# RWKV chunk inversion: odd chunks swap the heads' halves at each product, and the inverse is built from factors of one plus a power

## What is computed

```python
def step(s, inp):
    r_t, w_t, k_t, v_t, a_t, b_t = inp
    sa = jnp.einsum('bhij,bhj->bhi', s, a_t)
    s = s * w_t[:, :, None, :] + sa[..., None] * b_t[:, :, None, :] + v_t[..., None] * k_t[:, :, None, :]
    return s, jnp.einsum('bhij,bhj->bhi', s, r_t)
```

## Time and profile before

| what | value |
|---|---|
| median of 3 runs | 4082.98 us |
| range of the 3 runs | 4081.25 to 4083.41 us |
| profiled execution, own time | 4082.34 us |
| span of the profiled execution | 4080.1 us |
| instructions in the span | 84733 |
| PE busy, share of the span | 94% |
| DVE busy, share of the span | 58% |
| ACT busy, share of the span | 38% |

### The profile page before, as it was taken

The page is one execution under the profiler, slowest core; times in us unless marked ns, Lnnn a source line. Parts: engine busy times, 40 slices in busy tenths (PEclk is TensorE's granted clock), DMA queues, the critical chain, the costliest instruction groups (busy, mean ns, idle before and its releaser), DMA issues. The chain is left out here.

```text
span 4080.1 us, 84733 instructions
## 1 busy us (share of the span) xinstructions
PE 3834.2 (94%) x35926; PEld 3513.7 (86%) x35926; DVE 2363.4 (58%) x4633; ACT 1554.1 (38%) x2889; POOL 195.1 (5%) x203
## 2 busy tenths in 40 slices
PE   8999999999999999889978999979999999999998
PEld 4889999998888889889976777769876899999997
DVE  4445656432588885348976777646643564444446
ACT  3113222232386653334325666544522531111112
POOL 0000000000011111010000000001111100000000
PEclk9999999999999999999999999989999999999999
DMA  5323223243465544655641111052323121111112
GB/s 210 92 88 91 93 83 96 79 117 120 156 143 167 147 135 137 179 152 179 223 165 34 38 37 42 20 178 86 114 91 118 64 89 46 42 52 42 42 32 86
DMA packets 375542, 418.70 MB, mean 103 GB/s; under 512 B 50474, under 2 KB 317276, under 8 KB 374300
## 3 DMA queue, kind: packets, MB, share of 16 engines
q1 hardware_dynamic: 362927, 368.14, 29.3%
q0 software_dynamic: 7632, 27.84, 2.2%
q10 hardware_dynamic: 4608, 17.30, 1.1%
HBM read 289.10 MB, written 121.77 MB: 101 GB/s over the span
## 5 line engine op out<-in xcount | busy, mean ns | idle before, releaser
L248 PE MATMUL bank<-xn_hi,pw_whi 128*128 128x352 f32 (+1 forms) x2184 | 730.0, 334 | 14.0 <-ACT ring L261 6.2
L248 PE MATMUL bank<-xn_hi,pw_wlo 128*128 128x352 f32 (+1 forms) x2184 | 707.2, 324 | 0.0
L248 PE MATMUL bank<-xn_lo,pw_whi 128*128 128x352 f32 (+1 forms) x2184 | 706.2, 323 | 0.0
L248 PEld LDWEIGHTS bank<-xn_hi,pw_whi 128*128 128x128 f32 (+1 forms) x2184 | 412.8, 189 | 37.2 <-issue 23.1
L248 PEld LDWEIGHTS bank<-xn_lo,pw_whi 128*128 128x128 f32 (+1 forms) x2184 | 414.1, 190 | 3.1 <-issue 1.9
L248 PEld LDWEIGHTS bank<-xn_hi,pw_wlo 128*128 128x128 f32 (+1 forms) x2184 | 412.7, 189 | 1.3
L261 ACT ACTIVATE ring<-bank 128x352 f32<-128x352 f32 (+1 forms) x273 | 126.0, 462 | 439.0 <-PE bank L248 438.4
L3196 PE MATMUL bank<-bx_hi,bp_whi 128*128 128x384 f32 (+1 forms) x768 | 269.8, 351 | 19.0 <-DVE bx_lo L3257 16.8
L1786 PE MATMUL bank<-sum_x_hi,pw_whi 128*128 128x352 f32 x768 | 254.2, 331 | 32.8 <-DVE sum_x_lo L1777 13.9
L233 DVE TENSOR_TENSOR pw_wlo<-ring,pw_whi 128x1024 fp32r<-128x1024 f32 (+1 forms) x92 | 117.6, 1279 | 241.4 <-ACT pw_whi L226 241.0
L3833 PE MATMUL bank<-bx_hi,bp_whi 128*128 128x384 f32 (+1 forms) x768 | 251.2, 327 | 4.7 <-issue 4.7
(11 more groups left out here) (699 smaller groups left out, 10202.2 us busy)
## 6 DMA issues: line engine op xcount, KB each, us to landing
ring<-in_w_in_dram SPq DMA_DIRECT2D x90, 512.0 KB, 4.6
proj_scratch<-ring SPq DMA_DIRECT2D x66, 528.0 KB, 2.9
mm_all<-proj_scratch SPq DMA_DIRECT2D x40, 512.0 KB, 5.9
mm_all<-acum_scratch SPq DMA_DIRECT2D x32, 512.0 KB, 6.6
ring<-in_mlp_w_dram SPq DMA_DIRECT2D x16, 1024.0 KB, 5.5
ring<-in_mlp_w_dram SPq DMA_DIRECT2D x32, 512.0 KB, 3.4
gates_scratch<-ring SPq DMA_DIRECT2D x24, 528.0 KB, 6.6
merged_scratch<-sum_gate ACTq DMA_DIRECT2D x24, 528.0 KB, 4.9
```

Source lines behind the costliest of these rows:

```text
L248: last = self.nc.tensor.matmul(ps[0:n, 0:m], w[:, q, 0:n], self.pair[x][:, q, t0:t0 + m], start=q == 0 and j == 0, stop=q == KD - 1 and j ...
```

## The change

Four things are changed.

1. **Corners.** Of the four chunks of a set, the even ones still use `heads`. The odd ones use `swapped` in each product from `square` to `cross1`, so that their heads' halves change places at each step. Results of even chunks go to the set's first bank, of odd chunks to the second, and a copy reads both banks in one instruction. Within a step the order is chunk by chunk, each with all of its products.
2. **Factors.** `fourth` also forms a product of factors; X is never added. DVE makes each factor as power plus one (`plus_one`), and a later product multiplies it in. The number of steps falls from 11 to 10. `rows_vd` gets one more product for odd chunks (A with its halves swapped), `eighth` takes over what the old `by8` needed, `turn` and `cross1` get one more product for each chunk, and `cross3` goes.
3. **Who copies.** ACT copies two or three results at once: 512 columns in `square`, 768 in `fourth` and in `turn`, none in `eighth`. DVE now takes part in `rows_vd`. Where both engines take part, DVE waits until ACT has ended its copy, and its piece stands a slot later (`STEPS_V`).
4. **Slots.** Each step's slot is now a number in the list. `fourth` stands in slots 10 and 11 (before 9 and 10), `turn` in 17 and 18 (before 15 and 16), `cross1` in 20 and 21 and `cross2` in 22 and 23. Slots 2, 9, 12 and 19 have no piece of `Invert` on PE.

```diff
-INVERSION = [("gram", "v"), ("rows_kb", "a"), ("rows_vd", "a"), ("square", "va"), ("fourth", "va"), ("eighth", "va"), ("by8", "v"),
-             ("turn", "va"), ("cross1", "v"), ("cross2", "v"), ("cross3", "v")]
+INVERSION = [("gram", "v", 0), ("rows_kb", "a", 3), ("rows_vd", "va", 5), ("square", "va", 7), ("fourth", "va", 10), ("eighth", "v", 13),
+             ("by8", "v", 15), ("turn", "va", 17), ("cross1", "v", 20), ("cross2", "v", 22)]
+STEPS = {at + p: (s, p) for s, (_, _, at) in enumerate(INVERSION) for p in range(2)}
+STEPS_V = {at + p + ("a" in who): (s, p) for s, (_, who, at) in enumerate(INVERSION) if "v" in who for p in range(2)}
...
+            q, odd = i // 2, i % 2
+            e = 2 * odd + q
+            out = lambda n: (b1 if odd else b0)[:, n * P + q * RC:n * P + (q + 1) * RC]
+            corner = swapped if odd else heads
...
             elif step == "square":
-                heads(mm, b0[:, q], A, x.D[:, i, :], start=True, stop=True)
-                last = heads(mm, b1[:, q], x.D[:, i, :], A, start=True, stop=True)
+                corner(mm, out(0), A, x.D[:, e, :], start=True, stop=True)
+                last = corner(mm, out(1), x.D[:, e, :], A, start=True, stop=True)
             elif step == "fourth":
-                heads(mm, b0[:, q2], x.A2[:, i, :], x.DY[:, i, :], start=True, stop=True)
-                last = heads(mm, b1[:, q], x.DY[:, i, 0:RC], x.A2[:, i, :], start=True, stop=True)
+                corner(mm, out(0), x.A[:, e, :], x.D[:, e, :], start=True, stop=True)
+                corner(mm, out(1), x.D[:, e, :], x.A[:, e, :], start=True, stop=True)
+                last = corner(mm, out(2), x.P[:, e, :], x.X[:, e, :], start=True, stop=True)
...
+        plus_one = lambda t, n: tt(halves(t), self.product(p, n), v.eye2[:, :].unsqueeze(1).broadcast_to([P, 2, P]), ALU.add)
...
+        if "a" in INVERSION[s][1]:
+            dve.wait_ge(self.as_[p], evacuated(r, s, "a"))
+        else:
+            dve.wait_ge(self.pes[p], r * len(INVERSION) + s + 1)
...
         elif step == "square":
-            last = copy(x.A2[:, :, :], b1)
+            last = copies(x.DA, 0, 2)
         elif step == "fourth":
-            last = copy(x.A4[:, :, :], b1)
-        elif step == "eighth":
-            last = copy(x.A8[:, :, :], b1)
+            last = copies(x.DAX, 0, 3)
         else:
-            last = copy(x.G[:, :, :], b1)
+            last = copies(x.FGE, 0, 3)
```

## The result

The changed kernel takes 4114.79 us (median of 4 runs, 4111.05 to 4122.74) where the kernel before takes 4082.73. The ratio is 1.0082, 95% interval 1.0064 to 1.0099: **slower by 0.8%, about 33 us**. The forecast was 4072 us, with a range from 4032 to 4106.

The account below looks back on a forecast made before the run. The prediction took a chain through in-order engines as the bound: fourteen rounds at -0.5 us (-7), first round -1.5 and last -3, together -11.5 us, giving 4072 us, range 4032 to 4106.

Parts of the forecast that it names:

- What bounds the kernel: In the stage's rounds: a chain through in-order engines, PE, ACT or DVE longest by slot, not PE alone; 31.85 us a round.
- What PE saves: `square` to the end: even and odd chunks side by side save 20 turns, 2.34 us a set, 75 us of PE time.
- What the round gets: Each full round: stretches sum to -0.8 us covered, -0.3 at worst; -0.5 taken, -7 us over fourteen rounds.
- slots 9 to 12: Behind ST: shorter PE work, though wide ACT copies delay U and ST; 4.29 falls to about 3.2 us, gain 1.1.
- slots 12 to 15: DVE's 2.5 us of operations and a `by8` copy precede R; 3.26 grows to about 4.1 us, loss 0.9.
- slots 15 to the next round: `cross3` goes and `turn` costs less, against wide ACT copies and two more DVE operations ahead of R; gain 0.7 us.
- the case with the three-product steps late: Whole round: three-product steps finish late and `rows_vd` is uncovered, so the round gains only 0.3 us.
- the first rival: Whole stage: wide copies hide better, PE's savings return; half is -2.8 us a round, 4038 us (4008 to 4058); chance 0.20.
- The step that failed first: the clock: Idle PE in slots 8 and 9 halves its clock, slowing slots 10 to 12; 21 us, 4104 us; chance 0.07.
- the supply of instructions: New four-corner steps: 0.28 us gaps as PE's instructions run dry, half counted, 1.7 us a round; 4102 us; chance 0.20.
- The start: First round, with no scan beside it, only the chain of steps: -1.5 us, between 0 and -4.
- The round without `Prepare`: Last inverting round, no ACT block, so PE's work counts: 27.39 us, 4.7 saved at most, -3 taken.

Follow-up runs that it names:

- e5: Changed kernel plus three pairs of unread filler products on PE in slot 9, with all inversion products on the two corners of `heads`: 4140.54 us.
- e1: Changed kernel plus three pairs of unread 448-column filler products on PE in slot 9, ahead of its wait for ST: 4095.89 us.
- e4: Kernel before the change, with all its steps from `fourth` on one slot later, leaving PE an empty slot 9: 4111.27 us.
- e6: Changed kernel with three filler pairs in slot 9 and DVE's pieces of `Prepare` moved from slots 14 to 18 to 15 to 19: 4095.30 us.

## Why the prediction was wrong

The forecast was 4072 us and faster; the kernel is 0.8% slower. By its own steps:

**What bounds the kernel: right.** PE at 94% busy was not the limit. Its busy time fell from 30.00 to 28.65 us a round, and the round got longer.

**What PE saves: right in kind, too large.** The corners do run side by side, in 0.70 to 0.88 us for a step with three products (I took 0.8), and are worth 45 us when the clock is held (e5). But with the clock held and the filler taken off, PE is busy 27.0 us a round: 3.0 saved, where I counted 4.7. The Trainium skill's rule that matmuls start and end strictly in program order ("TensorE: Matmul & The Clock Gate", "Part 3: Packing small matmuls") does not hold here: R starts at 2329.92 ahead of records of `fourth` that precede it.

**What the round gets.** Forecast and measured change of each stretch against the kernel before, mean of 13 rounds, in us:

| stretch | forecast | e1, clock held | changed kernel |
|---|---|---|---|
| slots 6 to 9 | 0 to -0.1 | -0.01 | -0.08 |
| slots 9 to 12 | -1.1 | -0.85 | +0.32 |
| slots 12 to 15 | +0.9 | +1.13 | +1.64 |
| slots 15 to the next round | -0.7 | -0.05 | -0.06 |
| slots 0 to 6 | 0 to +0.2 | +0.38 | +0.27 |
| round | -0.5 | +0.61 | +2.09 |

The forecast stretches add up to a gain of 0.7 to 1.0 us; my -0.5 lies between that and the -0.3 of the case with the three-product steps late. A second slip changed nothing: half of the 4.7 us in the first rival is 2.35, not 2.8.

The DVE rows of slots 13 to 15 in the kernel after answer to the earlier trace rows, and they are the sum I made, 2.5 us of evacuations and wide operations and a `by8` copy ahead of R:

```profile
2340.90 0.42 DVE L1365 TENSOR_TENSOR r_inv<-bank,r_eye 128x256 f32<-128x256 f32 x1 [0.69 <-PE bank L1138]
2341.24 0.41 DVE L1382 COPY r_inv<-bank 128x256 f32<-128x256 f32 x1
2341.57 0.68 DVE L1269 TENSOR_TENSOR r_bonus<-bank,r_V 128x512 f32<-128x512 f32 x1
2342.17 0.41 DVE L1365 TENSOR_TENSOR r_inv<-bank,r_eye 128x256 f32<-128x256 f32 x1
2342.50 0.41 DVE L1382 COPY r_inv<-bank 128x256 f32<-128x256 f32 x1
2342.83 0.68 DVE L1273 TENSOR_TENSOR r_AR<-r_pm,r_ex 128x512 f32<-128x512 f32 x1
2343.43 0.41 DVE L1384 COPY r_inv<-bank 128x256 f32<-128x256 f32 x1
2343.76 0.21 DVE L1496 COPY r_R<-bank 128x64 f32<-128x64 f32 x1
```

**The step that failed first: the clock.** The text named the mechanism, the place and nearly 3 us of idle time (2.70 measured), and then gave it a chance of 0.07 and no place in the sum, because the clock held for 3 to 5 us of light work in the last chunks. That row was no evidence for this case: here PE does nothing at all for over two microseconds. The size was near: I had 2 us on the chain for a fall, and it is 1.5 us a round against e1. What made even the rival's 4104 too low is the 0.5 of gain that I set against it, which didn't exist. The Trainium skill, "TensorE: Matmul & The Clock Gate", section "HAM oscillation — how this bites in real kernels", describes a fall at each idle stretch between bursts. The trace agrees in kind in 14 rounds of 14, though the waits in the page's example are 3 to 5 us long and here 2.4 to 2.7 us were enough.

**The second: the gain of the round itself.** With the clock held the round is not 0.5 shorter but 0.61 longer. The largest part is the stretch from slot 15 on. The -0.7 there turned out as -0.05 with the clock held. Its typical value in e1 is 12.0 us against 12.3 before, so 0.3 of the 0.7 came and the rest was mis-sized: slots 18 to 21 take 3.62, where the kernel before has 3.13, with two more DVE operations and ACT's second wide copy in the way. What came is lost to irregular delays.

**The third: the supply of instructions.** As a rival it had 0.20 and a price of 1.7 us a round. Measured is less, but not nothing: over the 13 rounds the gaps with no releaser are 0.36 us a round before, 0.51 in the changed kernel and 0.68 in e1, whose filler adds instructions. They are not the neat 0.28 us in each four-corner step of the earlier trace rows but gaps of up to 1.3 us here and there. The mean round of e1 is 0.37 above the sum of its typical stretches, that of the kernel before 0.04.

**The ends of the stage.** The start came out right: the first R copy is 1.4 us earlier (I had 1.5). The round without `Prepare` did not: -3 forecast, 29.52 against 27.39 measured, +2.1. It has no ACT block and no fall of the clock, but gaps without a releaser of 3.6 us against 1.4, one of them 1.67 in `rows_vd`. That fits the supply theory in part only: e5 has 31.08 there with 0.6 us of such gaps, and no corners. No run tested this round by itself, so its cause stays open.

So of the 2.09 us a round 1.48 go to the clock, shown by e1 and, on the other kernel, by e4. The other 0.61 is the balance, with the clock held, of the corners' gain of 3.03 (e5) against all the rest of the change. Of it 0.3 at most is the supply, by the gaps of e1, if all of them lay on the chain; 0.6 us in slots 12 to 15 is DVE's order, of which the round got back only half when that was changed (e6). How the remainder divides between wide copies, further DVE operations and slots is not shown.

## What to carry to other kernels

Taking work off PE can cost PE its clock: before moving work out of a stretch in which another engine holds the chain, look how long PE would then stand still, and put work there. Real work is better than work for nobody, but measure it: 0.8 us of it was not enough here. Packing four corners shortens the steps as the count of products says, but it uses up instructions faster, so that PE can run out of them, and it makes evacuation the next item. Look also at what stands ahead of a narrow copy of the serial chain on an in-order engine; putting that copy first was worth about 4 us on either kernel, which is within the noise.

## What the runs showed of the hardware

- PE's clock fell to 1.2 GHz behind 2.4 to 2.7 us of idle time, once in each of 14 rounds, while PE was busy 84% of the 400 us as a whole. A fall cost 1.6 us (e4). Behind 2.12 us it fell in ten rounds and held in three (e4).
- 2.47 us of products that nobody reads, in that idle time, kept the clock at 2.4 GHz in all rounds and made the kernel faster by 0.6%. One third of them kept it in 12 of 14.
- 36 more small matmuls a round, with 0.2 us more of PE time, raised PE's gaps without a releaser from 9.0 to 20.7 us in 400 us and, with four falls of the clock, the time by 24.5 us.
- Such gaps of PE, up to 1.6 us long, end 1.2 to 1.6 us after a 16 KB packet of the instruction queue has ended (224 of 225 in 14 traces).
- A corner of the array can start a later product while another still works on earlier ones: 0.12 us ahead in `fourth` (e1: 2329.92 against 2330.04).
- ACT copies 768 columns in 0.81 us, 0.71 from start to start, where 0.80 and 0.68 were estimated from narrower ones.
